# First layer of a decoder trunk: new places for key roots, key transposes, probability combinations and the memory load

## The reference, cut to what matters

```python
h = rms_norm(x, norm_mix[l])
qkv = (h @ w_in[l]).reshape(B, S, 3, N_HEADS_MIX, HEAD_DIM)
q, k, v = qkv[:, :, 0], qkv[:, :, 1], qkv[:, :, 2]
...
qa = diff_qk_prep(q[:, :, :a_end], qn_diff[l], positions)     # rms norm per half head, rotary
ka = diff_qk_prep(k[:, :, :a_end], kn_diff[l], positions)
o_a = diff_attention(...)                                     # softmax(q1 k1) - lam * softmax(q2 k2), times v
...
mix = jnp.concatenate([o_a, o_b, o_c], axis=2)
x = x + mix.reshape(B, S, MIX_WIDTH) @ w_out[l]
x = x + memory_cross_attention(rms_norm(x, norm_cross[l]), rms_norm(mem, norm_mem[l]), ...)
x = x + swiglu(rms_norm(x, norm_ffn[l]), w_gate_up[l], w_down[l])
```

## Time and profile before

| | |
|---|---|
| three runs | 692.95, 694.41, 695.4 us (median 694.41) |
| the profiled execution | 694.24 us, its span 692.4 us |
| TensorE busy | 676.7 us (98%) |
| VectorE busy | 499.0 us (72%) |
| ScalarE busy | 393.4 us (57%) |
| GpSimd busy | 102.1 us (15%) |

### The profile page before, as it was taken

The page is one execution under the profiler, slowest core; times in us unless marked ns, Lnnn a source line. Parts: engine busy times, 40 slices in busy tenths (PEclk is TensorE's granted clock), DMA queues, the critical chain, the costliest instruction groups (busy, mean ns, idle before and its releaser), DMA issues.

```text
span 692.4 us, 10599 instructions
## 1 busy us (share of the span) xinstructions
PE 676.7 (98%) x3706; PEld 562.8 (81%) x3706; DVE 499.0 (72%) x953; ACT 393.4 (57%) x641; POOL 102.1 (15%) x117
## 2 busy tenths in 40 slices
PE   8978999999999999999999999999999999999997
PEld 7756787787888888888888877778788888888886
DVE  7658877778766666666678798875877666666665
ACT  7747686467544444444467569774774444444442
POOL 3262002208000000000032430202540000000000
PEclk9989899999999999999999999999999999999999
DMA  9943732243666666666555545213475666666631
GB/s 335 340 168 123 241 126 91 92 122 118 188 199 198 193 193 187 182 182 182 183 183 193 195 125 182 97 61 103 101 224 166 198 193 195 194 196 190 182 122 61
DMA packets 121903, 117.74 MB, mean 170 GB/s; under 512 B 2832, under 2 KB 95632, under 8 KB 121744
## 3 DMA queue, kind: packets, MB, share of 16 engines
q1 hardware_dynamic: 121296, 116.27, 54.3%
q10 hardware_dynamic: 576, 1.06, 0.4%
HBM read 116.28 MB, written 1.05 MB: 169 GB/s over the span
## 4 chain that ended last, share of the span: by engine, by line
PE 81%; ACT 7%; DVE 6%; DMA 3%; issue 1%; POOL 1%; SPq 1%; DVEq 0%; POOLq 0%
PE ps L2053 22%; PE ps L1671 14%; PE ps L2060 12%; PE ps L2101 6%; PE ps L2102 6%; PE ps L2103 6%; PE ps L1744 3%; DMA raw<-in_w_in 3%; ACT sq L765 2%; PE ps L2082 2%; DVE wlo L985 2%; PE ps L1986 2%; PE ps L1819 2%; PE ps L1855 1%; ACT whi L651 1%; PE ps L1561 1%
## 5 line engine op out<-in xcount | busy, mean ns | idle before, releaser
L985 DVE TENSOR_TENSOR wlo<-raw,whi 128x2048 fp32r<-128x2048 f32 (+1 forms) x93 | 207.2, 2245 | 44.8 <-ACT whi L649 44.2
L649 ACT ACTIVATE whi<-raw 128x2048 fp32r<-128x2048 f32 (+1 forms) x100 | 185.0, 1875 | 15.7 <-PE ps L2103 7.7
L2053 PE MATMUL ps<-both,whi 128*128 128x512 f32 x672 | 167.2, 391 | 0.0
L2053 PEld LDWEIGHTS ps<-both,whi 128*128 128x128 f32 x672 | 123.4, 188 | 23.8
L2060 PEld LDWEIGHTS ps<-both,wlo 128*128 128x128 f32 x672 | 91.7, 190 | 6.5
L1671 PE MATMUL ps<-whi,both 128*128 128x512 f32 x352 | 94.1, 405 | 0.4 <-ACT qkv L728 0.3
L2060 PE MATMUL ps<-both,wlo 128*128 128x256 f32 x672 | 94.1, 283 | 0.0
L923 ACT ACTIVATE qkv<-ps 128x512 f32<-128x512 f32 x42 | 25.1, 597 | 110.5 <-PE ps L2060 110.5
L1671 PEld LDWEIGHTS ps<-whi,both 128*128 128x128 f32 x352 | 66.9, 194 | 15.4 <-issue 1.1
L2101 PE MATMUL ps<-whi,ahi 128*128 128x512 f32 x176 | 69.2, 393 | 0.0
L2102 PE MATMUL ps<-wlo,ahi 128*128 128x512 f32 x176 | 69.0, 392 | 0.0
(11 more groups left out here) (220 smaller groups left out, 899.4 us busy)
## 6 DMA issues: line engine op xcount, KB each, us to landing
raw<-in_w_gate_up SPq DMA_DIRECT2D x88, 512.0 KB, 4.9
raw<-in_w_down SPq DMA_DIRECT2D x22, 1024.0 KB, 5.0
raw<-in_w_in SPq DMA_DIRECT2D x20, 1024.0 KB, 5.1
raw<-in_w_out SPq DMA_DIRECT2D x8, 1024.0 KB, 5.1
raw<-in_w_mkv SPq DMA_DIRECT2D x4, 1024.0 KB, 5.4
raw<-in_w_in SPq DMA_DIRECT2D x8, 256.0 KB, 4.8
raw<-in_w_in SPq DMA_DIRECT2D x4, 512.0 KB, 9.0
raw<-in_w_mq SPq DMA_DIRECT2D x4, 512.0 KB, 3.4
```

The lines of the kernel that those rows point to most:

```text
L649: ins = act.activation(whi[s][:, cols], raw[s][:, cols], ACT.Copy)
L985: ins = dve.tensor_tensor(wlo[s][:, cols], raw[s][:, cols], hi, ALU.subtract)
L2053: pe.matmul(ps[:, bank, :], whi[s][:, a:a + P], both[:, :, k, :], start=(k == 0), stop=False)
```

## The change

Six things, all in layer 0; layer 1 has the values that it had.

1. VectorE: norm_k of the first keys moves from step 14 to 13, and so ahead of the low part of unit 4, which moves from 13 to 14 (its high part from 12 to 13 on ScalarE, behind the sine). The low part of unit 5 moves from 19 to 25, that of unit 6 from 25 to 26, behind the query roots. The high part of unit 5 moves from 18 to 24.
2. TensorE: for units 4 and 5 the products with low x come ahead of those with low w.
3. The first keys' transposes move from step 32 to 36; the second keys' roots from 41 to 37; the second queries' from 53 to 54; low parts of units 7 and 8 to 36 and 38.
4. Memory's high parts go to steps 40, 41, 42, 55 and its low parts to 44, 44, 57, 57, so that the last two no longer stand ahead of combine(0) and combine(1), at step 49.
5. The load of the memory's rows is started behind both w_mkv loads, squares of it at 71 in place of 60, roots asked for at 75 and taken at 77 in place of both at 65.
6. Low parts of units 12, 13, 14 move to 66, 70, 75 (from 61, 67, 73).

```diff
--- before.py
+++ after.py
@@ -450,12 +450,11 @@
                         load(layer, u, [(view(u, 4), w_in[:, 4 * h:4 * h + 4, cols])])
                         if layer == 0 and u == MEM_COLUMNS_AFTER:
                             sp.dma_start(mem_sb[:].rearrange("p t d -> p (t d)"), consts["mem_columns"]).then_inc(s_memT.sem, 16)
-                        if layer == 0 and u == MEM_AFTER:
-
-                            sp.wait_ge(m_lo.sem, 4)
-                            sp.dma_start(mem_sb[:], mem.rearrange("b (t p) d -> p (b t) d", p=P)).then_inc(s_mem.sem, 16)
                 for h in range(2):
                     load(layer, U_MKV + h, [(view(U_MKV + h, 4), w_mkv[:, 4 * h:4 * h + 4, :])])
+                if layer == 0:
+                        sp.wait_ge(m_lo.sem, 4)
+                        sp.dma_start(mem_sb[:], mem.rearrange("b (t p) d -> p (b t) d", p=P)).then_inc(s_mem.sem, 16)
                 for h in range(2):
                     for c in range(2):
                         u = U_OUT + 2 * h + c
@@ -814,13 +813,13 @@
                         if g == 12 * NCHUNK + 9 + 3 * t:
                             mkv_tile(t)
                     for q in range(4):
-                        if layer == 0 and g == MEM_AT[q]:
+                        if layer == 0 and g == MEM_HI_AT[q]:
                             mem_hi(q)
                     for m in range(HEADS):
                         if g == T_AT[m]:
                             probT_out(m)
                     for e in range(4):
-                        if g == QKT_AT[e]:
+                        if g == QKT_AT[layer][e]:
                             qkT_out(e)
                     for d in range(DUOS):
                         for b in range(2):
@@ -1304,7 +1303,7 @@
 
                 for g in range(6, LAST + 1):
                     for q in range(4):
-                        if layer == 0 and g == MEM_AT[q]:
+                        if layer == 0 and g == MEM_LO_AT[q]:
                             mem_lo_part(q)
                     for d in range(DUOS):
                         if g == S_AT[d]:
@@ -1326,10 +1325,11 @@
                     if layer == 0 and g == MEM_ROOT_AT:
                         dve.wait_ge(s_memss.sem, 1)
                         ask_root(dve.tensor_scalar(nv[:, 0:T], mem_ss[:], 1.0 / D, EPS, ALU.mult, ALU.add))
+                    if g == SUB_AT:
+                        sub_norm()
+                    if layer == 0 and g == MEM_ROOT_AT + 2:
                         take_root()
                         dve.tensor_copy(mem_r[:], ny[:, 0:T]).then_inc(s_memr.sem, 1)
-                    if g == SUB_AT:
-                        sub_norm()
                     for m in range(DIFF, HEADS):
                         if g == N_AT[m - DIFF]:
                             divide(m)
@@ -1649,7 +1649,7 @@
 
                     s = u % RING
                     hi, lo = sources
-                    if u == 1 or layer == 0 and u in (2, 3):
+                    if u == 1 or layer == 0 and u in (2, 3, 4, 5):
                         x_part, w_part = ((hi, whi), (lo, whi), (hi, wlo))[part]
                     else:
                         x_part, w_part = ((hi, whi), (hi, wlo), (lo, whi))[part]
@@ -1713,7 +1713,7 @@
                         h, t = t, h
                     elif c == 0:
                         return
-                    elif layer == 0 and c == 1:
+                    elif layer == 0 and c in (1, 2):
                         t, part = THIRD_PIECES[p % 6]
                     if c < NCHUNK:
                         proj_piece(c, h, t, part)
@@ -2128,21 +2128,24 @@
 OUT1_EARLY = ((0, 0), (1, 0), (0, 1))
 WARM = 7
 X_COLUMN_LOADS = ((0, (1, 2)), (1, (2, 4)), (3, (4, 6)), (5, (6, 8)))
-MEM_COLUMNS_AFTER, MEM_AFTER = 7, 11
+MEM_COLUMNS_AFTER = 7
 THIRD_PIECES = ((0, 0), (0, 1), (1, 0), (1, 1), (0, 2), (1, 2))
 SIN_AT = 12
 TABLE_AT = 14
 QK_CHUNKS = (0, 1, 2, 3)
 
 
-CHAIN_AT = ((14, 25, 41, 53), (14, 26, 45, 53))
+CHAIN_AT = ((13, 25, 37, 54), (14, 26, 45, 53))
 LO_AT = [[6 * (u - 2) + 1 for u in range(3, U_MQ)] for _ in range(DEPTH)]
-LO_AT[0][7 - 3], LO_AT[0][9 - 3], LO_AT[0][10 - 3] = 37, 46, 50
+LO_AT[0][7 - 3], LO_AT[0][8 - 3], LO_AT[0][9 - 3], LO_AT[0][10 - 3] = 36, 38, 46, 50
 HI_AT = [[6 * (u - 2) for u in range(3, U_MQ)] for _ in range(DEPTH)]
 HI_AT[0][9 - 3] = 44
-HI_AT[0][4 - 3], LO_AT[0][4 - 3] = 12, 13
+HI_AT[0][4 - 3], LO_AT[0][4 - 3] = 13, 14
+HI_AT[0][5 - 3], LO_AT[0][5 - 3] = 24, 25
+LO_AT[0][6 - 3] = 26
+LO_AT[0][12 - 3], LO_AT[0][13 - 3], LO_AT[0][14 - 3] = 66, 70, 75
 QKT_DVE_AT = ((None, None, None, 71), (32, 43, None, 71))
-QKT_AT = (32, 43, 64, 71)
+QKT_AT = ((36, 43, 64, 71), (32, 43, 64, 71))
 COMBINE_AFTER = (4, 3, 4, 7)
 S_AT = (45, 46, 54, 54, 66, 69, 73, 77, 82, 86)
 SCORES_AT = (45, 45, 54, 54, 66, 69, 73, 77, 81, 86)
@@ -2153,14 +2156,14 @@
 SUMS = [(0, 0, 0), (0, 0, 1), (1, 0, 0), (1, 0, 1), (1, 1, 0), (2, 0, 0), (2, 0, 1), (2, 1, 0)]
 SUB_AT = 76
 STORES = ((0, 0, 512), (0, 512, 1024), (1, 0, 512), (1, 512, 768), (1, 768, 1024))
-MEM_AT = (40, 47, 48, 49)
-MEM_SQ_AT = 60
+MEM_HI_AT, MEM_LO_AT = (40, 41, 42, 55), (44, 44, 57, 57)
+MEM_SQ_AT = 71
 HB_AT = (81, 81, 90)
 KM_AT = 94
 N_BUILD = 1
 N_AT = (69, 70, 72, 74, 76, 78, 80, 80, 85, 85, 89, 90)
 LAM_AT, LAM_EXP_AT = 38, 44
-MEM_ROOT_AT = 65
+MEM_ROOT_AT = 75
 LAST = max(FILLERS + 3 * len(OUT1_EARLY) - 1, V_AT[-1])
 
 
```

## The result

The changed kernel took 682.17 us (median of 4 runs, 681.57 to 682.75) against 693.68 us before (4 runs, 692.72 to 695.4): a ratio of 0.9831, 95% interval 0.9808 to 0.9855, 11.5 us less by the medians. The two profiled executions are 12.7 us apart: 694.24 and 681.57. The first of these is above the median of its kernel and the second is the fastest of its four, so the medians are the fairer measure. The forecast was 681.2, a gain of 13.2 us on a median before of 694.41.

A forecast was written before the change was run, and what follows sets the result against it. TensorE was taken as the bound, nearly always busy: 9.2 us of waits plus 4.9 of slow clock, 14.1, less 0.85 of new waits, gives 13.2 us gained, forecast 681.2 us; 8-in-10 range 679.5 to 686.8.

The forecast's parts named there:

- The gain from waits and clock: Steps 24 to 77: 9.2 us of TensorE waits plus 4.9 us of slow clock, 14.1 us at most to win.
- 0.25, 0.1 and 0.3: New TensorE waits in us: unit 4's low part (step 28), unit 6's low part (step 37), the queries' transposes (step 43).
- 0.2 at step 73: New wait of 0.2 us allowed for the second half of the query copies, behind unit 13's low part.
- Part 1: First keys' roots ahead of unit 4's low part: keys ready at 29.15 against 33.5, rotated at 36.5; 0.25 us new wait.
- Part 2: Key transposes at step 36, not 32: the 4.0 us wait and its clock fall go; 0.1 and 0.3 us new waits.
- Part 3: Combinations ahead of memory's low parts: combine(0) ends at 56.9, TensorE arrives at 58.5, the 3.3 us wait goes.
- Part 4: Memory's squares and roots are covered by more than 3 us; its load moves past both w_mkv loads; cost nothing.
- rival D: SP's wait for the fourth memory low part delays all w_out loads, making the kernel slower; chance 0.03.
- the orders are as before: After step 77 nothing changes in the orders, so the 13.2 us gain was carried to the end.
- A: GpSimd held longer by VectorE: queries at 49.8, TensorE waits 3.8 us at step 43, 2.2 slow clock; 686.7; chance 0.10.
- B: VectorE late: waits of 1 to 1.5 us return at three places without slow clock, 3.2 us more, 684.4; chance 0.12.
- C: The first keys come no sooner, only parts 3 and 4 win; 688; chance 0.03.

The follow-up runs named there:

- e4: Kernel before, with 15 and 12 idle matmuls ahead of the first key transposes and first probability transpose; no wait removed: 691.78 us, ratio 0.9981 to before.
- e2: Changed kernel with the first keys' roots behind unit 4's low part again, transposes still at step 36: 683.07 us.
- e3: Changed kernel with the first keys' transposes back at step 32: 682.75 us.
- e7: Changed kernel with the edits of e2 and e3 together, roots behind unit 4's low part and key transposes at step 32: 683.71 us.
- e1: Changed kernel with memory's high and low parts back at steps 40, 47, 48, 49: 687.07 us.
- e6: Kernel before with only memory's high parts at 40, 41, 42, 55 and low parts at 44, 44, 57, 57, load not moved: 701.44 us, ratio 1.0119.
- e10: Changed kernel, memory's last low parts at 60, units 13 and 14's at 71 and 79, first heads' squares and sums and memory roots at 73: 679.47 us.
- e12: Changed kernel with VectorE's low parts of units 6 and 7 each made by two instructions of half the size: 682.04 us.
- e11: The changed kernel again, nothing changed, timed beside other runs: 681.90 us.
- e8: Changed kernel, memory's last low parts at 60, units 13 and 14's at 71 and 78, memory squares at 76, roots from 78: 683.26 us.
- e9: Kernel before with memory's parts at the new steps, its load behind the w_mkv loads, squares at 71, roots at 75: 690.37 us.
- e5: Changed kernel with the old order of products in units 4 and 5, high x with low w second: 683.61 us.

## Why the prediction was right, point by point

**The gain from waits and clock.** Right at the place where I summed it: 14.1 us at most from step 24 to 77, 13.2 forecast, 13.8 measured. But the terms do not match one by one. The 14.1 us were not the most that could be won: start against start the waits before cost 10.0 us, where their idle times sum to 9.2 (the first, at 29.67, costs 29.67 - 27.56 - 0.91 = 1.2 for 1.0), so the stretch held 14.9. And the new waits were not those of the sum: 0.25, 0.1 and 0.3 did not come, 0.2 at step 73 was 0.5, and 0.5 for the third combination came unforeseen, together 1.1 start against start where the sum had 0.85. 14.9 - 1.1 is the 13.8 measured, 0.6 more than the sum; that these 0.6 make up for part of what was lost behind step 77 is luck. e4 shows that the sum was safer than its reasoning: waits and slow clock add up only if no other engine is late behind them. In the kernel before it was. The change also took VectorE's idle time out:

```profile
49.66 1.22 DVE L1154 TENSOR_REDUCE g<-sqc 128x16 f32<-128x1024 f32 x1 [7.11 <-ACT sqc L738]
```

This is the kernel before, 7.1 us of idle time ahead of the second key sums; in the changed kernel no row of VectorE from 25 to 77 us shows idle time ahead of it. I take this to be what let the whole sum be collected; no run shows it by itself. Where the clock was the only thing mended (e4), 1.5 to 3.0 of the 4.9 us came.

**Part 1, roots ahead.** The roots ended at 28.8 (29.15 worked out), the low part of unit 4 at 31.0 (31.4), the keys were rotated at 36.2 (36.5). The wait of 0.25 at step 28 did not come. But the attribution was too simple, so for this wait the right size is partly luck. I gave the 4.0 us to these roots and to the later transposes; e2, e3 and e7 show that either one nearly suffices beside the moved low parts, and that the roots' own worth (0.9 us by medians of different sets) lies in VectorE's queue.

**Part 2, transposes at 36.** TensorE came at 38.55 (38.7). The queries: rotation worked out to end at 46.0, seen at 45.4, TensorE at 45.9: no wait where I had put 0.3. GpSimd was held by both low parts, but one operation passed with each, so 2 of the 8 operations of the rotation, 0.9 us of work, were done by then; I had allowed 0.4.

**Part 3, combinations.** combine(0) from 56.8 to 57.9 (forecast end 56.9), TensorE at 58.9 (58.5). The terms written for that 58.5 add up to 58.0, so the margin on paper was 1.1 us and not 1.6; 0.9 was left. e1 prices it at 4.9 us, with 6.0 in my sum (3.3 + 2.7). The third combination was in truth late, by 0.46 us: VectorE's queue was 71.1 on paper and ended at 72.8. VectorE did not idle there; its jobs were longer than summed. Up to combine(0) they took 33.8 us for 32.8, above all the low parts of units 6 and 7 (4.9 for 4.4) and the second key roots (3.6 for 3.0); behind it 14.9 for 14.2, above all the second combination (1.8 for 1.1). GpSimd was at work beside all three. So a wait that I had at zero.

**Part 4, memory.** "Cost nothing" was right for the loads of the kernel as changed (the first w_out load was issued at 72.3, and ScalarE, which converts it at 86.8, did not wait) and wrong as a description. The move of the load is no free extra, it is what part 3 needs: without it e6 loses 9 us. My rival D had the mechanism, SP's wait with loads queued behind it, but I looked only at the new queue (w_out) and not at what the old one (w_mkv) would have suffered.

**After step 77.** The step of the sum that failed, and the largest miss in it: "the orders are as before". They are, but their surroundings are not. Counted from step 77, unit 14's low part came 1.1 us later than before and the first heads' variance 0.9 later (VectorE's sum for it waited another 0.35 us for ScalarE), so GpSimd's norm (94.1 on) fell beside VectorE's copy of the roots (0.92 us for 2 columns) and a pair of divisions that took 1.57 us (0.55 undisturbed), and step 79 waited 0.7; its two transposes, parted by the wait, take 1.55 us in place of 0.63. So 0.9 us were lost that the sum did not have. With 13.8 gained up to step 77, 0.1 more ahead of step 24 and 0.2 more behind step 84, the profiled span shrinks by 12.6 us; the sum said 13.2. e10, which moves the squares, the norm and unit 14's low part apart again, takes 13.2 us from step 77 to step 84 as the kernel before does, against 14.15 in the changed kernel. By the medians the gain is 11.5; the median before was 0.7 lower than the one that the forecast started from, and the changed kernel 1.0 above the forecast.

**The rivals.** A did not come, for two reasons: two operations passed with the low parts where A had none (e12 and e11 show that one passes per instruction), and VectorE came to the key product at 46.3 and not at 45.6, when the rotation was through. On the row and the Trainium skill's rule (GPSIMD Engine Reference, Key points): the contention with VectorE instructions of two SBUF inputs is there, in all low parts; the key product, by which rival A was made worse, had no GpSimd work beside it (the rotation had ended at 45.4, the product ran from 46.3). B came in small, as waits of 0.5 us. C and D did not.

## What to carry to other kernels

A gap of TensorE that is cured by an order has often several covers; undo them one at a time and together before giving one of them the credit: here two edits came to 0.9 and 0.6 us of a gap that cost 6.2 with its slow clock. When a job is moved on one engine, look at what another queue holds behind its semaphore, and move that too: the place of a load, with the squares and roots behind it, was worth 11 us here. When VectorE is 95% full in a stretch, waits of half a microsecond can hang on which of its jobs lies ahead (e8, e10), and GpSimd's list behind it belongs to the same order.

## What the runs showed of the hardware

GpSimd, beside VectorE's subtractions of two SBUF operands, gets one operation through for each VectorE instruction: 2.4 us each with 2048 columns, 1.2 to 1.4 with 1024 (e12), where the same operations take 0.3 to 0.5 us by themselves. In the other direction, in the changed kernel's profile, a VectorE copy of 2 columns took 0.92 us beside a GpSimd product of 512 (0.17 in the kernel before, with nothing beside it), and a pair of divisions 1.57 in place of 0.55.

The granted clock fell to 0.50 at waits of TensorE of 8.9 us (e6), 4.0 (before, e6 and e9), 3.3 (before) and 3.0 (e1), and stayed at 1.00 at waits of 2.1 us (e8), 1.2 (e3), 1.0 (e7) and less. It also stayed at 1.00 where matmuls without use filled the waits of 4.0 and 3.3 (e4).

The time at which TensorE reached step 24 varied from 27.4 to 29.6 us over fourteen profiles; in a late one (e5) four products begun at 8.65 us took 1.9 us where later ones take 1.1, in an early one (e10) four begun at 7.35 took 1.1 already, while the windows of e5 gave the clock as 1.00 from the start. No run looked for the cause.
